# Block 1's attentions: scores of two pairs in two places of three banks, probabilities turned through one bank in pieces

## The reference

```python
ya = window_attention_latent(rope(qa), rope(ka), va, kac, vac, sink_a[l])   # 8 heads of 64, 2 key heads
yb = full_attention_latent(rope(qb), rope(kb), vb, kbc, vbc)                # 8 heads of 64, 2 key heads
if not last:                                                              # layer 0 only
    yac = context_attention(qac, kac, vac, N_KV_A, sink_a[l])
    ybc = context_attention(qbc, kbc, vbc, N_KV_B, None)
```

## Time and profile before

| | us |
|---|---|
| median of 3 runs | 3474.71 (3474.41 to 3478.57) |
| the profiled execution | 3481.14 |
| its span | 3479.2 |
| attentions of layer 0, from the first scores to GpSimd's last split | 290.3 to 482.7 |
| attentions of layer 1, the same | 1375.4 to 1535.4 |

### The profile page before, as it was taken

One profiled execution on the slowest core, in us unless ns is written; L12 is line 12 of the kernel. 1 busy time (PEld: TensorE's weight loads), 2 busy tenths in 40 slices (PEclk: granted clock), 3 DMA queues, 4 the chain that ended last, 5 costly groups with the idle time before them and its releaser, 6 DMA issues. The chain is left out here.

```text
span 3479.2 us, 49806 instructions
## 1 busy us (share of the span) xinstructions
PE 3310.0 (95%) x20432; PEld 2653.7 (76%) x20432; DVE 1807.0 (52%) x2942; ACT 1210.4 (35%) x2054; POOL 445.8 (13%) x477
## 2 busy tenths in 40 slices
PE   6998899999999999889999999899999998899998
PEld 4887678788888787666787867667888777578886
DVE  5875767654232466765323357664443385734433
ACT  3214763311131222763223333353322332533322
POOL 0211111000000021113600133120000022200000
PEclk9999999999999999999999999999999999999999
DMA  6420013354212122012222321012223320022232
GB/s 241 146 103 14 1 45 130 120 197 146 65 63 73 49 86 72 1 37 88 97 92 96 103 85 62 20 43 91 97 91 103 103 85 3 31 91 97 91 102 80
DMA packets 78266, 290.67 MB, mean 84 GB/s; under 512 B 8672, under 2 KB 9056, under 8 KB 77280
## 3 DMA queue, kind: packets, MB, share of 16 engines
q1 hardware_dynamic: 78048, 287.55, 24.3%
HBM read 285.42 MB, written 2.10 MB: 83 GB/s over the span
## 5 line engine op out<-in xcount | busy, mean ns | idle before, releaser
L459 DVE TENSOR_TENSOR w_low<-ring,w_high 128x1024 fp32r<-128x1024 f32 x418 | 526.8, 1260 | 1350.8 <-ACT w_high L456 1350.1
L494 PE MATMUL ps<-arena_r,w_high 128*128 128x512 f32 x3568 | 1143.8, 386 | 10.4 <-PEq L1515 9.1
L456 ACT ACTIVATE w_high<-ring 128x1024 fp32r<-128x1024 f32 x418 | 442.9, 1060 | 1517.6 <-PE ps L494 1508.5
L494 PEld LDWEIGHTS ps<-arena_r,w_high 128*128 128x128 f32 x3568 | 646.8, 188 | 163.6 <-issue 16.9
L494 PE MATMUL ps<-low,w_high 128*128 128x512 f32 (+1 forms) x2448 | 765.2, 361 | 0.0
L494 PE MATMUL ps<-high,w_high 128*128 128x512 f32 x2368 | 737.1, 362 | 15.1 <-DVE low L992 6.9
L494 PE MATMUL ps<-high,w_low 128*128 128x512 f32 x2368 | 730.9, 359 | 0.0
L494 PE MATMUL ps<-arena_r,w_low 128*128 128x512 f32 (+1 forms) x1456 | 546.3, 388 | 0.0
L494 PEld LDWEIGHTS ps<-low,w_high 128*128 128x128 f32 x2448 | 412.1, 189 | 74.9 <-issue 1.2
L494 PEld LDWEIGHTS ps<-high,w_high 128*128 128x128 f32 x2368 | 395.4, 189 | 95.4 <-issue 12.0
L494 PEld LDWEIGHTS ps<-high,w_low 128*128 128x128 f32 x2368 | 395.1, 188 | 70.5
(11 more groups left out here) (353 smaller groups left out, 2941.4 us busy)
## 6 DMA issues: line engine op xcount, KB each, us to landing
ring<-in_weights SPq DMA_DIRECT2D x428, 512.0 KB, 3.3
arena<-in_ada_rows SPq DMA_DIRECT2D x80, 512.0 KB, 3.9
arena<-in_ada SPq DMA_DIRECT2D x16, 512.0 KB, 15.7
arena<-in_cond_rows SPq DMA_DIRECT2D x3, 1024.0 KB, 5.9
xL<-in_x SPq DMA_DIRECT2D x1, 2048.0 KB, 10.4
out<-xL SPq DMA_DIRECT2D x4, 512.0 KB, 2.7
low_f<-in_low_rank SPq DMA_DIRECT2D x3, 512.0 KB, 4.3
const<-in_const SPq DMA_DIRECT2D x1, 1104.0 KB, 5.4
```

Of the source, the lines that this page charges most:

```text
L456: act.activation(w_high[:, slot, :], ring[:, place, :], ACT.Copy).then_inc(unit_high.sem, 1)
L459: dve.tensor_tensor(w_low[:, slot, :], ring[:, place, :], w_high[:, slot, :].bitcast(F32), ALU.subtract).then_inc(unit_free.sem, 1)
L494: mm = pe.matmul(bank(4 * (t % 2) + 2 * p + s, width), w, g.split[k][s][x], start=(n == 0 and m == 0), stop=(n == len(part) - 1 and m == 2))
```

## The change

A new function `attention_by_bank` takes the place of `attention` in the first block. It needs no new data and leaves the other call alone.

- Scores of a pair take three banks, both heads one behind the other (head 1 at column 768 of the place, or at 512 for pairs of at most 512 keys), and there are two such places, used in turn. Scores of pair i wait for the exponentials of pair i-2. Where the heads share the middle bank, the second writer waits for the first (`shared_bank`), and for B the second head's keys are cut 256, 512 instead of 512, 256.
- Probabilities of both heads lie packed, and are turned through one bank in pieces of 512 columns: three pieces for 640 and 768 keys (the last of 640 is 256 wide), two for 512, one for 256. Each piece waits for the copy of the one before.
- TensorE's order in iteration i: first piece of pair i-1, scores of pair i+1, second piece, values of pair i-2, third piece.
- VectorE's order: `normalize` of pair i-1, `maxima` of pair i+1. 
- ScalarE's order: exponential of head 0 of pair i, first piece of pair i-1, exponential of head 1, second piece, sinks, heads of pair i-2, third piece. For pairs above 512 keys the first exponential waits for both maxima.

```diff
--- before.py
+++ after.py
@@ -1694,6 +1694,204 @@
                          (heads_in, 1), (heads_out, int(bool(beside)))):
                 c.base += m * n
 
+        shared_bank = count("shared_bank")
+        def attention_by_bank(pairs, scale, heads_on_vector=False):
+            n = len(pairs)
+            T_AT, O_AT = 6 * BANK, 7 * BANK
+            chunks = [-(-2 * pair["keys"] // BANK) for pair in pairs]
+            chunk0 = [sum(chunks[:i]) for i in range(n + 1)]
+            def scores_at(i, e):
+                return (i % 2) * 3 * BANK + e * (T if pairs[i]["keys"] > BANK else BANK)
+            def sinks(i):
+                return sum(pair["sink"] is not None for pair in pairs[:i])
+            def large(i):
+                return sum(pair["keys"] > BANK for pair in pairs[:i])
+            def flat(i):
+                return probs[:, i % 3].rearrange("p e t -> p (e t)")
+            def of_head(i, e):
+                return flat(i)[:, e * pairs[i]["keys"]:(e + 1) * pairs[i]["keys"]]
+            def chunk(i, c):
+                return c * BANK, min((c + 1) * BANK, 2 * pairs[i]["keys"])
+            with nc.Block() as block:
+                @block.tensor
+                def _(pe):
+                    def scores(i):
+                        pair = pairs[i]
+                        if i >= 2:
+                            pe.wait_ge(exp_out.sem, exp_out.at(2 * (i - 2) + 2))
+                        for c in range(len(pair["scores"][0])):
+                            for f in ((0, 1) if c % 2 == 0 else (1, 0)):
+                                q, k, at, w = pair["scores"][f][c]
+                                to = scores_at(i, f) + at
+                                shared = pair["keys"] > BANK and (f, c) == (0, len(pair["scores"][0]) - 1)
+                                if shared:
+                                    pe.wait_ge(shared_bank.sem, shared_bank.at(large(i + 1)))
+                                mm = pe.matmul(ps[:, to:to + w], q, k, start=True, stop=True)
+                                if pair["keys"] > BANK and (f, c) == (1, 0):
+                                    mm.then_inc(shared_bank.sem, 1)
+                        mm.then_inc(scores_in.sem, 2)
+                    def turn(j, c):
+                        first, end = chunk(j, c)
+                        pe.wait_ge(probs_out.sem, probs_out.at(2 * j + (1 if end <= pairs[j]["keys"] else 2)))
+                        if chunk0[j] + c:
+                            pe.wait_ge(turned_out.sem, turned_out.at(chunk0[j] + c))
+                        for at in range(first, end, P):
+                            to = T_AT + at - first
+                            mm = pe.transpose(ps[:, to:to + P], flat(j)[:, at:at + P], con("ident"))
+                        mm.then_inc(turned_in.sem, 1)
+                    def values(j):
+                        pair = pairs[j]
+                        pe.wait_ge(turned_out.sem, turned_out.at(chunk0[j + 1]))
+                        if j:
+                            pe.wait_ge(heads_copied.sem, heads_copied.at(j))
+                        tiles = pair["keys"] // P
+                        for m in range(tiles):
+                            for e in range(2):
+                                mm = pe.matmul(ps[e * HD:e * HD + HD, O_AT:O_AT + P], pair["values"][e][m],
+                                               of_head(j, e)[:, m * P:m * P + P], start=(m == 0), stop=(m == tiles - 1))
+                        mm.then_inc(heads_in.sem, 1)
+                    scores(0)
+                    scores(1)
+                    for i in range(1, n + 2):
+                        j = i - 1
+                        if j < n:
+                            turn(j, 0)
+                        if i + 1 < n:
+                            scores(i + 1)
+                        if j < n and chunks[j] > 1:
+                            turn(j, 1)
+                        if j >= 1:
+                            values(j - 1)
+                        if j < n and chunks[j] > 2:
+                            turn(j, 2)
+                @block.vector
+                def _(dve):
+                    def maxima(i):
+                        pair = pairs[i]
+                        st, keys = stat[:, 8 * (i % 4):8 * (i % 4) + 8], pair["keys"]
+                        dve.wait_ge(scores_in.sem, scores_in.at(2 * i + 2))
+                        for e in range(2):
+                            part = ps[:, scores_at(i, e):scores_at(i, e) + keys]
...
+                    def normalize(j):
+                        pair, st = pairs[j], stat[:, 8 * (j % 4):8 * (j % 4) + 8]
+                        dve.wait_ge(exp_out.sem, exp_out.at(2 * j + 2))
+                        if pair["sink"] is not None:
+                            dve.wait_ge(sinks_out.sem, sinks_out.at(sinks(j + 1)))
+                            chain_v.link(dve, dve.tensor_tensor(st[:, 4:6], st[:, 4:6], st[:, 6:8], ALU.add))
+                        chain_v.link(dve, dve.reciprocal(st[:, 4:6], st[:, 4:6]))
+                        for e in range(2):
+                            p = of_head(j, e)
+                            dve.tensor_scalar(p, p, st[:, 4 + e:5 + e], None, ALU.mult).then_inc(probs_out.sem, 1)
+                    def heads(j):
+                        dve.wait_ge(heads_in.sem, heads_in.at(j + 1))
+                        dve.tensor_copy(pairs[j]["y"], ps[:, O_AT:O_AT + P]).then_inc(heads_copied.sem, 1)
+                    maxima(0)
+                    for i in range(n + 3):
+                        if 0 <= i - 1 < n:
+                            normalize(i - 1)
+                        if heads_on_vector and i >= 3:
+                            heads(i - 3)
+                        if i == n:
+                            split_unit(None, dve, 0, 0, None, 0)
+                            split_unit(None, dve, 1, 1, None, 0)
+                        if i + 1 < n:
+                            maxima(i + 1)
+                @block.scalar
+                def _(act):
+                    def copy(j, c):
+                        first, end = chunk(j, c)
+                        act.wait_ge(turned_in.sem, turned_in.at(chunk0[j] + c + 1))
+                        act.activation(flat(j)[:, first:end], ps[:, T_AT:T_AT + end - first], ACT.Copy).then_inc(turned_out.sem, 1)
+                    def exponent(i, e):
+                        pair, st = pairs[i], stat[:, 8 * (i % 4):8 * (i % 4) + 8]
+                        act.wait_ge(max_out.sem, max_out.at(2 * i + (2 if pair["keys"] > BANK else e + 1)))
+                        if i >= 3:
+                            act.wait_ge(heads_in.sem, heads_in.at(i - 2))
+                        act.activation(of_head(i, e), ps[:, scores_at(i, e):scores_at(i, e) + pair["keys"]],
+                                       ACT.Exp, bias=st[:, 2 + e:3 + e], scale=scale,
+                                       accum_out=st[:, 4 + e:5 + e]).then_inc(exp_out.sem, 1)
+                    def sink(i):
+                        pair, st = pairs[i], stat[:, 8 * (i % 4):8 * (i % 4) + 8]
+                        for e in range(2):
+                            ins = act.activation(st[:, 6 + e:7 + e], pair["sink"][e][0], ACT.Exp, bias=st[:, 2 + e:3 + e])
+                        ins.then_inc(sinks_out.sem, 1)
+                    def heads(j):
+                        act.wait_ge(heads_in.sem, heads_in.at(j + 1))
+                        act.activation(pairs[j]["y"], ps[:, O_AT:O_AT + P], ACT.Copy).then_inc(heads_copied.sem, 1)
+                    for i in range(n + 2):
+                        j = i - 1
+                        if i < n:
+                            exponent(i, 0)
+                        if 0 <= j < n:
+                            copy(j, 0)
+                        if i < n:
+                            exponent(i, 1)
+                        if i == n:
+                            split_unit(act, None, 0, 0, None, 0)
+                        if 0 <= j < n and chunks[j] > 1:
+                            copy(j, 1)
+                        if i < n and pairs[i]["sink"] is not None:
+                            sink(i)
+                        if i >= 2 and not heads_on_vector:
+                            heads(i - 2)
+                        if 0 <= j < n and chunks[j] > 2:
+                            copy(j, 2)
+                        if i == n:
+                            split_unit(act, None, 1, 1, None, 0)
...
+            heads_copied.base += n
+            sinks_out.base += sinks(n)
+            shared_bank.base += large(n)
+            turned_in.base += chunk0[n]
+            turned_out.base += chunk0[n]
+            for c, m in ((scores_in, 2), (max_out, 2), (exp_out, 2), (probs_out, 2), (heads_in, 1)):
+                c.base += m * n
         def pairs1(l):
 
             pairs, own = [], []
@@ -1718,8 +1916,8 @@
```

(6 more changed lines are left out.)

18 lines of the change are left out of this document (added).

## The result

The changed kernel takes 3552.31 us (median of 4 runs, 3547.97 to 3557.56), the one before 3476.64 on the same chip (4 runs, 3474.41 to 3481.52). The ratio is 1.0216, with an interval of 1.0196 to 1.0237: 76 us slower, where I said 49, and 2 us above the top of my range. The profiled execution took 3557.56 (span 3555.3, mean granted clock 0.982). The ratios of this document leave out two executions in a much slower state, 11880.84 us among those of experiment 6 and 3749.69 us among those of the kernel before beside experiments 5 to 7.

A forecast was written before the change was run, and what follows sets the result against it. It took a ring of scores, maxima and exponential to bound window pairs, VectorE the own pairs. 21.3 + 22.7 - 1.4 + 3.3 + 2.5 + 0.7 = 49.1 us took profiled 3481.1 to 3530, median forecast 3524; 80% range 3503 to 3550.

The forecast's parts named there:

- the ring: Window pairs: first piece, scores, maxima, first scaling, TensorE's wake-up in sequence; 5.35 and 5.01 us (640 keys), 5.28 and 4.52 (512).
- The `shared_bank` wait is on a matmul issued two before: hidden: Scores of 768-key pairs: the second writer's wait for the bank both heads share adds no time.
- I take nothing: Scores of 768-key pairs: 512 columns beside 256 priced at zero, with 14 us kept as a rival.
- Rival 1: Scores of 768-key pairs: unequal halves wait for each other, 0.43 us per pair, 14 us in all, 3538; chance 0.20.
- The first scaling: Term in the window pairs' ring, on VectorE: 0.62, 0.55 and 0.48 us for 768, 640 and 512 keys.
- rival 3: Window pairs: TensorE's own work binds, not the ring through the scaling; 23 us go, 3452; chance 0.09.
- The ring through the copies: Window pairs: the one bank for turned pieces and its copies; 5.36 us for 768 keys, 4.9 for 640.
- Own pairs, +22.7: Context's own pairs: VectorE stands still 1.51 us each time, two pairs take 6.95 instead of 3.93; +22.7 us over 15 steps.
- rival 2: Own pairs: TensorE's clock falls between pieces, 1.0 us longer in each of 16, +16, 3540; chance 0.10.
- ScalarE isn't late anywhere: Window pairs: ScalarE's work is 3.4 us of an iteration of 4.5 to 5.4.
- Window pairs together: From the fifth maxima to the last, 27 pairs in each of two layers: 0.39 us per pair more, +21.3 us.
- The ends and starts: Attention blocks' edges: starts -1.4 us, layer 1's end +3.3, layer 0's end +2.5, passage to own pairs +0.7.

The follow-up runs named there:

- experiment 6: Changed kernel with 768-key pairs cut evenly, scores split around the first piece, own pairs' exponentials and sinks ahead of the copy: 3482.43 us, ratio 1.0011.
- experiment 5: Changed kernel with six unused matmuls behind the values of each of the context's own pairs: 3546.95 us, ratio 1.0199.
- experiment 7: The kernel of experiment 6 with GpSimd's split of a pair waiting for the scaling of the pair two further on: 3480.09 us, ratio 0.9999.
- Experiment 8: The kernel of experiment 7 with two of three score parts of 768-key pairs ahead of the first piece, instead of one: 3475.13 us, ratio 0.9994.
- experiment 1: Changed kernel with the keys of 768-key pairs cut 256, 256, 256 for both heads: 3538.50 us, ratio 1.0166.
- experiment 4: Changed kernel with GpSimd's split of a pair also waiting for the scalings of the pair two further on: 3540.11 us, ratio 1.0186.
- experiment 2: Changed kernel with TensorE issuing the next pair's scores ahead of the first piece: 3529.84 us, ratio 1.0149.
- experiment 9: The kernel of experiment 7 with all score parts but the last ahead of the first piece, for all window pairs: 3476.02 us, ratio 0.9997.

## Why the prediction was wrong

The direction and the ring were right. One cost that I set to nothing was real, one scaling was too short, the clock fell in part of the own pairs, and a third ring was missed, which the change as it stands doesn't show.

- **The ring.** As written. A's scores with B's scaling: 4.96 against 5.01, term by term (piece to scores 0.58, scores to maxima 1.40, maxima to reciprocal 2.11, reciprocal to the next piece 0.87). VectorE wakes TensorE in 0.06 (the first of the two scalings from 363.08 took 0.83; the piece starts at 363.97); I took 0.10. B's scores with A's scaling: 5.98 against 5.35, which is 0.40 for the scores and 0.28 for the scaling, less 0.04 for the wake-up. Experiment 8, which changes only one cut, orders and one wait of GpSimd around that ring, gives all 76 us back.
- **The step that failed first: "The `shared_bank` wait is on a matmul issued two before: hidden", and with it "I take nothing" for the unequal halves.** B's scores took 1.96 and not 1.56, and experiment 1 gave back 14 us. The wait was not hidden. Its increment came only when the wider matmul issued before it was over, and held head 0's last matmul back by 0.32 (359.54 to 359.86); the last two instructions then stand 0.29 apart instead of 0.22. I had both prices, 0 and 0.43, and no row near either; the rows being silent was a reason to weigh them alike, not to take zero. Rival 1 had the price right and its mechanism only in part: a half does not wait for the other to go on, it only signals no earlier. That the 0.39 comes so near to its 0.43 is in part luck. The Trainium skill (TensorE: Matmul & The Clock Gate, section The mechanism) has matmuls start and end in the order of issue; for the ends this trace agrees, with the increment at 359.72 behind the wide matmul's end at 359.69.
- **The first scaling.** Its term, "0.62, 0.55 and, carried on, 0.48", was taken from rows in which GpSimd stands elsewhere. In the new order GpSimd's split of A's output falls on two of four of A's first scalings: 0.83 instead of 0.55 at 363.08. GpSimd gives way too: its CAST takes 0.68 beside the scaling at 357.31, and 0.29 at other places. Experiment 4 shows the cause; in the window pairs it was worth 4 us. The argument against rival 3, "VectorE's durations are those of instructions that already run beside ScalarE and TensorE", forgot this third neighbour. The Trainium skill (SBUF — State Buffer, section Who interferes with whom) says that VectorE's `tensor_scalar` can take a pair of ports that GpSimd also uses, and that whoever comes second then stands still. At 357.31 this trace agrees: the CAST starts 0.09 behind the scaling (357.40) and is the one that grows. At 363.08 the scaling grows by 0.28, though its row starts 0.03 ahead of the split's; start times of GpSimd are rough, so which came first stays open there.
- **The ring through the copies** I had at 5.36 for B beside 5.35. It was in truth level with the first, and binds where the first is eased: in one of eight pairs of the kernel after (TensorE then waits 0.56 for the copy), and in experiments 2, 4 and 9.
- **Own pairs, +22.7.** At 2.4 GHz they stand 3.37 to 3.63 apart, where I had 3.48, and in experiment 4, with the clock up throughout, they cost +22.2. But rival 2 came true as well: in three stretches (474.8 to 491.8, 502.1 to 512.3, and, at the block's end, 526 to 539.6) the granted clock is 0.50, and pairs there are 4.74 apart. That makes +31. My evidence against it, 476 to 482 before the change with 3.25 busy of 6 us, was one window of 6 us at the end of the block. The third ring, through ScalarE's order, I missed. In the kernel after it is hidden: 3.31 and 2.85 us in experiment 2, both below 3.37. "ScalarE isn't late anywhere" was read from its load, which is right, and not from its order.
- **Window pairs together:** 0.65 and not 0.39 for each of the 54, +35 for +21.3. Experiments 1 and 4 give 0.20 of it to the cut and 0.08 to the scaling, 0.02 more than the 0.26 that there is to explain.
- **The ends and starts.** Layer 1's end cost 5.1 (I had 3.3), partly because the clock fell there too (1597.7 to 1601.2), layer 0's 3.4 (2.5). The starts gave 4.1 (I had 1.4). The passage cost 0.2 (I had 0.7).
- **The range.** Rivals 1 and 2 were priced about right, at +14 and +16, and stood beside each other as if only one could be true. Both costs came, the second by half: 3524 + 14 + 8 = 3546. Of the 27 us by which the profiled execution lies above the forecast for it, the window pairs hold 13.7, the own pairs 8.4, and the stages outside the two blocks, for which I had nothing, 5.5; starts, ends and passage cancel but for 0.5. That the median lies only 2 us above the range is no merit of the range.

What stays open is what decides over the clock in the own pairs. Experiment 4 and the kernel after have nearly the same load there and idle times of the same size, and one execution in four of experiment 4 had the lower mean clock. In experiment 1, whose own pairs have the code of the kernel after, the clock was low from 468.2 to 509.1, and they stood 4.25 apart.

## What to carry to other kernels

When engines follow written orders, write each iteration as loops through all the orders, ScalarE's too, and not only through the engine that looks late: three rings lay within 0.5 us of each other here, and easing one alone gave at most 22 us of 76. A wait for one's own earlier matmul isn't hidden because it was issued two before: look at what was issued ahead of that one, and how long it lasts. Before turning one group of transposes into three, price the switches on the engine that will become the bound: of the 0.46 us of idle time that left each pair, the pieces and the parted scores took 0.42. And where a rival cost is independent of the others, its price belongs in a sum of several, not only beside the forecast.

## What the runs showed of the hardware

- Two matmuls beside each other on the halves of the array, 512 columns with 256: the narrow half goes on with its next matmul at once (359.11 beside 359.10), but the narrow one's semaphore increment comes only when the wide one issued before it is over (359.72, where its own end is modelled at 359.27). With a wait for it in the scores these took 1.96 us, with equal cuts 1.57.
- A scaling of 640 columns on VectorE, SBUF to SBUF, takes 0.55 us alone and up to 0.83 beside a GpSimd split; GpSimd's CAST goes from 0.29 to 0.68.
- TensorE's granted clock fell to 0.50 in own pairs whose idle gaps were under 2 us and whose load over 494 to 500 (3.01 of 6 us busy) went with 1.00; in another execution, of experiment 4, 30.41 of 52 us busy went with 1.00 throughout.
